# Hybrid decoder step on one core: Pool mixing in three rounded passes, and two token blocks of the second layer fetched and split in the last output tile

## The reference

```python
h = rms_norm(x, g);  z = h @ W_in            # layer 0: 4096 columns, layer 1: 7168
branch = pool_mix(u)            # layer 0: trailing mean over 16, 8, 4 or 2 rows, minus the row,
                                # then per group of 384 channels a 384x384 product, and a scale
branch = stick_breaking(q, k, v)                # layer 1
y = concat(branch * silu(gate), mem_attn(mq) * silu(mgate)) @ W_out;  x = x + y
```

## Time and profile before

| | |
|---|---|
| runs | 2331.37, 2334.32, 2334.16 us; median 2334.16 |
| profiled execution | 2338.4 us, span 2336.7 us |
| mean granted TensorE clock | 0.971 of 2.4 GHz |
| TensorE matmul busy | 2201.2 us (94%) |
| VectorE busy | 1292.6 us (55%) |
| ScalarE busy | 1009.2 us (43%) |
| GpSimd busy | 433.0 us (19%) |

### The profile page before, as it was taken

The page is one execution under the profiler, slowest core; times in us unless marked ns, Lnnn a source line. Parts: engine busy times, 40 slices in busy tenths (PEclk is TensorE's granted clock), DMA queues, the critical chain, the costliest instruction groups (busy, mean ns, idle before and its releaser), DMA issues. The chain is left out here.

```text
span 2336.7 us, 47103 instructions
## 1 busy us (share of the span) xinstructions
PE 2201.2 (94%) x18709; PEld 1834.6 (79%) x18709; DVE 1292.6 (55%) x2040; ACT 1009.2 (43%) x2090; POOL 433.0 (19%) x542
## 2 busy tenths in 40 slices
PE   7799999997999689999999998889999999998999
PEld 6799899886688589999999997766666566654787
DVE  6846666435422374334444443588888888875211
ACT  7533223215311144333333343457777777775100
POOL 0533223202000043222222221321121111100000
PEclk9899999998899889999999999889999999999999
DMA  8222222144635553334433336789999999978331
GB/s 289 86 87 89 79 64 66 66 166 163 210 119 155 146 186 102 109 99 133 153 106 109 96 96 234 253 292 379 396 407 393 406 395 388 375 284 307 123 108 55
DMA packets 283274, 453.98 MB, mean 194 GB/s; under 512 B 30962, under 2 KB 208062, under 8 KB 283038
## 3 DMA queue, kind: packets, MB, share of 16 engines
q1 hardware_dynamic: 274958, 421.83, 51.8%
q0 software_dynamic: 8000, 29.10, 3.3%
q10 hardware_dynamic: 96, 0.02, 0.0%
HBM read 372.43 MB, written 78.43 MB: 193 GB/s over the span
## 5 line engine op out<-in xcount | busy, mean ns | idle before, releaser
L233 DVE TENSOR_TENSOR h_w_lo<-l_w,h_w_hi 128x512 fp32r<-128x512 f32 x264 | 213.7, 811 | 221.2 <-ACT h_w_hi L226 218.7
L226 ACT ACTIVATE h_w_hi<-l_w 128x512 fp32r<-128x512 f32 x264 | 166.7, 633 | 239.9 <-PE i_c L322 81.4
L320 PE MATMUL i_x<-h_t_hi,h_w_hi 128*128 128x264 f32 x560 | 163.3, 292 | 6.8 <-DVE h_t_lo L279 6.8
L2960 PEld LDWEIGHTS b_krow<-ar_arena,b_qd 128*32 128x32 f32 x3072 | 107.2, 111 | 72.6 <-issue 57.0
L192 POOL TENSOR_TENSOR h_w_lo_full<-l_w 128x512 f32<-128x512 f32 x44 | 57.5, 1308 | 560.5 <-DMA l_w<-in_w_in_sb_dram 229.9
L320 PE MATMUL i_y<-h_t_hi,h_w_hi 128*128 128x264 f32 x560 | 161.3, 288 | 0.0
L322 PE MATMUL i_x<-h_t_hi,h_w_lo 128*128 128x264 f32 x560 | 161.0, 287 | 0.0
L321 PE MATMUL i_x<-h_t_lo,h_w_hi 128*128 128x264 f32 x560 | 160.4, 286 | 0.0
L321 PE MATMUL i_y<-h_t_lo,h_w_hi 128*128 128x264 f32 x560 | 159.0, 284 | 0.0
L322 PE MATMUL i_y<-h_t_hi,h_w_lo 128*128 128x264 f32 x560 | 158.9, 284 | 0.0
L2960 PE MATMUL b_krow<-ar_arena,b_qd 128*32 128x128 f32 x3072 | 140.7, 279 | 7.9 <-ACT b_kev L2666 6.9
(11 more groups left out here) (368 smaller groups left out, 6424.9 us busy)
## 6 DMA issues: line engine op xcount, KB each, us to landing
ar_arena<-in_cache_sb_k_dram SPq DMA_DIRECT2D x73, 768.0 KB, 9.7
bf_vpage<-in_cache_sb_v_dram SPq DMA_DIRECT2D x64, 768.0 KB, 8.8
b_vpage<-in_cache_sb_v_dram SPq DMA_DIRECT2D x64, 768.0 KB, 8.5
l_w<-in_w_in_sb_dram SPq DMA_DIRECT2D x56, 512.0 KB, 3.9
l_w<-in_cache_sb_k_dram SPq DMA_DIRECT2D x36, 768.0 KB, 9.4
l_w<-in_w_in_pool_dram SPq DMA_DIRECT2D x32, 512.0 KB, 4.2
bf_kpage<-in_cache_sb_k_dram SPq DMA_DIRECT2D x19, 768.0 KB
ar_arena<-scratch_yT SPq DMA_DIRECT2D x14, 1024.0 KB, 6.6
```

Of the source, the lines that this page charges most:

```text
L226: act.activation(self.w_hi[:, i % RING, :, :], self.source(i), ACT.Copy).then_inc(self.high, 1)
L233: dve.tensor_tensor(self.w_lo[:, i % RING, :, :], self.source(i), self.w_hi[:, i % RING, :, :].bitcast(F32), ALU.subtract).then_inc(self.r ...
L320: pe.matmul(out, w_hi, t_hi, start=kk == 0 and x in ("P1", "P2", "P5"), stop=False, skip_group_check=True)
L2960: ins = pe.matmul(krow[pair * CT:(pair + 1) * CT, 0:P], qd[:, i % 2, at:at + CT], kt[u % 2][:, h, f, :], start=odd == 0 and f == 0, stop=o ...
```

## The change

In layer 0 the ring of split weights has 6 places instead of 8 (5 products ahead instead of 7); the two free places hold the rounded mixing weights and the tail rows. The mixing is done in three rounded passes of 352 columns (81 matmuls a group instead of 27 fp32 ones). ScalarE rounds the mixing weights (`mix_weights`) and the pooled values in three pieces (`mix_high`), VectorE takes the rests (`mix_low`). The evictions go by token third first. `group(n)` moves behind P2 of the next group's first pair. The queries are fetched in two parts, head 0 only when the last mixing matmul is done.

In layer 1 the first pair begins P1, P2, P5. The first weights a(0), in a place of their own, and token blocks 0 and 1 are fetched in the last output tile, split by ScalarE and VectorE ahead of that tile's residual sum, and P1 and P2 run at the end of the output phase, the last tile's transposes between the two halves of P2. `in_phase` begins with P5.

```diff
@@ Quads
+        self.ring = PLACES if i else PLACES - 2
+        self.ahead = self.ring - 1
...
-            self.seq += [(p, "P5")] + [(p - 1, "P4")] * (p > 0) + [(p, x) for x in ("P1", "P2", "P6", "P3", "P7")]
+            begin = [(p, "P5"), (p - 1, "P4"), (p, "P1"), (p, "P2")] if p else [
+                (0, x) for x in (("P1", "P2", "P5") if i else ("P5", "P1", "P2"))]
+            self.seq += begin + [(p, x) for x in ("P6", "P3", "P7")]
@@ pool_phase, SyncE
-                memory.queries(sp)
+                memory.queries(sp, 1, MH)
+                memory.scales(sp)
+                sp.wait_ge(s["mready"], 9 * GROUPS)
+                memory.queries(sp, 0, 1)
                 memory.own_keys(sp)
@@ pool_phase, ScalarE
+                def mix_weights(n):
+                    act.wait_ge(s["wgl"], 16 * (n + 1))
+                    if n:
+                        act.wait_ge(s["mready"], 9 * n)
+                    for kk in range(GB):
+                        act.activation(wg_hi[kk], wg[:, kk, :], ACT.Copy).then_inc(s["wgh"], 1)
+
+                def mix_high(n):
+                    act.wait_ge(s["pooled"], GB * (n + 1))
+                    for u in range(NT):
+                        if u >= 2:
+                            act.wait_ge(s["mready"], 9 * n + 3 * (u - 1))
+                        act.activation(up_hi[u % 2], up[:, :, HIST + u * TT:HIST + (u + 1) * TT], ACT.Copy
+                                       ).then_inc(s["uph"], 1)
...
+                        for n in range(1, GROUPS):
+                            if p + 1 == first(n):
+                                mix_high(n - 1)
                         if p + 1 < q.n:
                             begin(p + 1)
...
+                mix_high(GROUPS - 1)
@@ pool_phase, VectorE
+                def mix_low(n, u):
+                    dve.wait_ge(s["uph"], NT * n + u + 1)
+                    cols = slice(HIST + u * TT, HIST + (u + 1) * TT)
+                    dve.tensor_tensor(up_lo[:, :, cols], up[:, :, cols], up_hi[u % 2].bitcast(F32), ALU.subtract
+                                      ).then_inc(s["upr"], 1)
@@ pool_phase, TensorE
-                                ins = pe.matmul(aux[(at + 1) % 2][:, 0:TT], wg[:, kk, m * P:(m + 1) * P],
-                                                up[:, kk, HIST + u * TT:HIST + (u + 1) * TT], start=kk == 0, stop=kk == GB - 1)
+                                cols, rows = slice(HIST + u * TT, HIST + (u + 1) * TT), slice(m * P, (m + 1) * P)
+                                ins = product3(pe, aux[(at + 1) % 2][:, 0:TT], wg_hi[kk][:, rows], wg_lo[:, kk, rows],
+                                               up_hi[u % 2][:, kk, :], up_lo[:, kk, cols], kk == 0, kk == GB - 1)
...
-                        if n and (p, x) == (first(n), "P1"):
+                        if n and (p, x) == (first(n), "P2"):
                             group(n - 1)
@@ out_phase, SyncE
+                        if t == N - 1:
+                            sp.wait_ge(s["ready"], 2 * (N - 1))
+                            sp.wait_ge(s["dead"], 1)
+                            q.load_a(sp, 0)
+                            for n in range(2):
+                                q.token_fetch(sp, S["tok"], n)
@@ out_phase, ScalarE and VectorE
+                    if norm and t == N - 2:
+                        act.wait_ge(s["dead"], 1)
+                        act.wait_ge(s["ready"], 2 * (N - 1))
+                        act.wait_ge(s["ylo"], N)
+                        for n in range(2):
+                            q.round(act, n)
+                            q.token_high(act, n)
...
+                    if norm and t == N - 2:
+                        for n in range(2):
+                            q.remainder(dve, n)
+                            q.token_rest(dve, n, n + 1)
@@ out_phase, TensorE
                 if norm:
+                    pe.wait_ge(s["added"], 2 * (N - 1))
+                    q.product(pe, 0)
+                    pe.wait_ge(s["sadded"], 1)
+                    q.product(pe, 1, range(1))
                     norm.turn(pe, N - 1)
+                    q.product(pe, 1, range(1, 2))
@@ in_phase
-                q.load_a(sp, 0)
-                for t in (0, 1):
-                    q.token_fetch(sp, S["tok"], t)
                 q.load_b(sp, 1)
...
-                for i, (p, x) in enumerate(q.seq):
+                for i, (p, x) in list(enumerate(q.seq))[2:]:
                     q.product(pe, i)
```

More of the change, by code:

```diff
@@ L217, in round @@
         p, x = self.seq[i]
-        if i >= RING:
-            act.wait_ge(self.done, 2 * (i - RING) + 2)
+        if i >= self.ring:
+            act.wait_ge(self.done, 2 * (i - self.ring) + 2)
         if x in ("P1", "P2"):
@@ L296, in tokens_vector, with product @@
             self.token_rest(dve, t, n)
-    def product(self, pe, i):
+    def product(self, pe, i, halves=range(2)):
         p, x = self.seq[i]
@@ L660, in _ @@
                 act.wait_ge(s["made"], 12)
-                for j in range(3):
+                for j in range(2):
                     q.round(act, j)
@@ L664, in _ @@
                 evacuate(7)
-                q.round(act, 3)
                 act.wait_ge(s["made"], 14)
-                for j in range(4, 6):
+                for j in range(2, 6):
                     q.round(act, j)
@@ L1028, in pool_phase @@
         state = k.sb("state", [NB_S * HIST, GW])
[L1029 removed]
+        tail = spare(q.w_full)[0:KEPT, GW:2 * GW]
         q.allocate_banks(k)
[L1031 to L1032 removed]
+        aux = q.aux
+        names = "gated zeroed keeps stl sturned wgl mready mixed pooled sums tailt tailc stored ystored carried wgh wgr uph upr".split()
         s = {n: k.sem(n) for n in names}
@@ L1070, in _ @@
                 for i, (p, x) in enumerate(q.seq):
-                    q.loads(sp, i + AHEAD - 1)
+                    q.loads(sp, i + q.ahead - 1)
                     if x == "P4" and p < 4:
@@ L1238, in _ @@
                 q.tokens_vector(dve, 0)
-                for j in range(6, AHEAD):
+                for j in range(6, q.ahead):
                     q.remainder(dve, j)
@@ L2105, in _ @@
                     q.token_fetch(sp, S["tok"], t)
-                for j in range(AHEAD - 1):
+                for j in range(q.ahead - 1):
                     q.loads(sp, j)
                 for i, (p, x) in enumerate(q.seq):
-                    q.loads(sp, i + AHEAD - 1)
+                    q.loads(sp, i + q.ahead - 1)
                     kind, h = kinds[p]
@@ L2142, in _ @@
             def _(gp):
-                for j in range(AHEAD + 1):
+                for j in range(q.ahead + 1):
                     q.combine(gp, j)
                 for i, (p, x) in enumerate(q.seq):
-                    q.combine(gp, i + AHEAD + 1)
+                    q.combine(gp, i + q.ahead + 1)
                     if (p, x) in ((0, "P4"), (1, "P4")):
```

226 lines of the change are left out of this document (144 added, 82 removed).

## The result

| | before | after |
|---|---|---|
| median | 2334.24 us (2331.4 to 2342.8) | 2360.28 us (2359.8 to 2361.6) |
| ratio, 95% interval | | 1.0119 [1.0098, 1.0139] |
| profiled execution | 2338.4 us, span 2336.7 | 2360.1 us, span 2358.4 |

What follows compares the result with a forecast made beforehand. TensorE, busy 2201 of 2337 us, was taken to bound the kernel. The terms -1 - 0.6 + 2 + 2.4 + 4.2 + 5 = +12.0 us on 2334.2 gave 2346 us, range 2333 to 2357.

Steps and rivals of the forecast that it cites:

- the join of the layers: Between output phase and second layer: stage starts 13.6 us later, 7.9 comes back; taken as +5 us (-1 to +8).
- what comes back: Second stage of layer 1: P7 27.0 us into the stage instead of 34.9, 7.9 us earlier (6 to 9).
- nothing catches up: Attention start: its own loads are issued behind the Pool stage's barrier, so the +4.2 us delay stays.
- The mixing itself: Pool stage mixing: 81 rounded matmuls at 0.16 us, 12.9 us a group instead of 16, 3.1 saved.
- The gain meets the state load: Pool groups 1 to 3: transposes wait for the state's load, leaving 0.2 us saved each, -0.6 us (-3.6 to +0.6).
- The clock behind the gaps: Behind Pool groups 1 to 3: 5 us gaps bring TensorE's half clock behind all three, +2 us (0 to +4).
- The last group: Last Pool mixing: starts 4.0 us late behind rounding, ends 0.9 late, begins at half clock, +2.4 us (0.5 to 3).
- the join to the attention: Pool stage end: head 0's fetch waits for the last mixing matmul, GpSimd's padding and barrier for it, +4.2 us.
- The Pool start: Start of Pool stage: with six ring places VectorE splits fewer weight blocks between awaited token blocks, -1 us (-2 to +1).
- The early fetches: Rival at the layer join: early fetches land at once and the joins hide, 2329 to 2333 us, chance 0.09.
- The shorter ring: Rival in the Pool stage: six ring places starve TensorE, adding 11 us, 2357 us, chance 0.07.
- The steady clock: Rival in the Pool stage: full clock after 5 us gaps, mixing 11.9 us a group, +2.6, 2337 us, chance 0.14.

Runs made afterwards that it cites:

- Run 2: The changed kernel with the Pool state fetched as soon as its buffer's transposes are done, ahead of the previous group's stores: 2344.6 us.
- run 8: The kernel before with the Pool state fetched ahead of the stores of the group before: 2323.4 us.
- run 3: The changed kernel with all four heads of queries fetched together before the last group: 2361.7 us.
- run 4: The changed kernel with all queries fetched before the last group and the own keys fetched behind that group's stores: 2355.3 us.
- run 6: The changed kernel with the early splits behind tile 7's square, norm and sums, and P1 and P2 at the second stage's start: 2348.2 us.
- run 7: The changed kernel, mended: state and all queries fetched early, own keys behind last stores, splits behind tile 7's chain, P1 and P2 in second stage: 2324.6 us.

## Why the prediction was right in direction and short in size

Set on the profiled executions, the terms are 9.7 us short. By the first table +5.5 lie in the join of the layers, +2.9 in the attention, +2.0 in groups 1 to 3 and +0.4 in the output phase, less 1.2 in the rest. Two steps failed in their mechanism, what comes back at the join of the layers and "nothing catches up" at the attention; in the others a size was off.

**The mixing itself, 12.9 us a group.** 13.65 us, 81 matmuls at 0.161 (forecast 0.16) and what remains until the last is done. The step held, 0.7 us short; against the 16.1 of the fp32 group 2.5 us are saved instead of 3.1.

**The gain meets the state load, -0.6 for three groups.** It held within its bounds (-3.6 to +0.6). From a group's first matmul to the transposes, with the 2.9 us of the product added, it was 22.1, 21.1 and 21.1 us (277.89 less 258.71, and so on), where 20.9 was forecast and 21.2, 21.7 and 21.0 stood before: +0.4. Run 2 shows the load to be the cause. I called the transposes bound by the load without asking why the load goes out so late; run 8 shows that question to be worth 10 us in the kernel before.

**The clock behind the gaps, +2.** The half clock came behind all three. The groups' stretch grew by 3.4 us, 0.4 of it the gap itself, which leaves 3.0 for the clock, inside the bounds of 0 to 4. Of these, 21 more matmuls at the half clock make 2.1; the slower transposes in front of them make up the rest.

**The last group, +2.4, and the join to the attention, +4.2.** Together 6.7 us, forecast 6.6, which is partly luck. The group started 4.1 us later behind the last product (forecast 4.0) and took 15.1 instead of 16.15, so it ended 3.0 late, and the join took 3.7 us more. The second term's reason was half of the truth: head 0's place was free (run 3), and the stores stood in the same queue. The step that failed is "the attention's own loads are issued behind this barrier, so nothing catches up": they are issued behind the landing of the last group's stores as well, and these had moved with the late fetches. Runs 3 and 4 show both halves. Missed: 2.9 us, part of it through the clock behind the longer wait.

**The join of the layers, +5.** It was +10.5, the largest miss. The way to the stage's start was right: 15.2 us later, forecast 13.6. The step that failed is what comes back. "P7 at 27.0, 7.9 us earlier" became 28.6, 6.3 earlier, and then 1.6 went to the wait at the next P5. I took token block 3 to be what P7 waits for and did not follow ScalarE's order through P5's copy, which holds the banks that P3 needs. P3 waited 3.57 us for that copy, P7 then ran right behind P3, and the next P5 waited 2.76 us for an addition of VectorE's. Of the miss of 5.5 us, 1.6 lie in the start, 1.6 in P7, 1.6 in the next P5, and 0.7 in rounding 5.7 down to 5 with "the rate may be a little better".

**The Pool start, -1.** -1.1 by the table, but not shown for its reason: TensorE's wait at the sixth product (P7) fell from 2.1 us to 0.35, and one of 1.8 for an addition of VectorE's came at 116.67, where the stage stood 0.5 us behind. The gain came later, from the clock: the same products took 1.4 us less, at 1.00 after the change and 0.95 before. No trace shows that the change has a part in that, so the agreement is luck. The stretch of before, then that of after:

```profile
164.50:198.00 33.50, 33.50 (x265) 33.50 (x265) 13.63 (x20) 17.65 (x33) 7.26 (x6) 0.95 0.30 95
```

```profile
164.90:197.00 32.10, 32.10 (x266) 32.10 (x266) 10.26 (x20) 17.44 (x32) 7.76 (x6) 1.00 0.35 118
```

**The base.** I subtracted the 4.2 us by which the profile of before lay above its runs. The profile after lies at its own median. The sum, set on the profiled execution, was 2350.4; measured 2360.1. So 9.7 us of the miss of 14 are terms, and 4.3 are this step. In which stages the profile of before lies above its own median is not shown.

**The rivals.** The early fetches did not land at once: weights at 813.4, block 0 at 816.1, 9.7 us behind the issue at 806.4, where 8.7 was forecast. The shorter ring starved nothing that the waits show; the ring was not run by itself. The steady clock did not come with gaps of 5 us.

## What to carry to other kernels

Where a wait is to be priced, ask first why its releaser starts when it does: three waits that I took as given were a fetch standing behind stores in one queue, and moving it alone was worth as much as the whole change, mended. An operation done early costs what stands behind it in every in-order queue that it passes, the stores' landing and the bank copies included; put it behind the chain that ends the phase, even if its data are there. And a stage's start is bound by all engines' last work before the barrier: when one late path is cut, the next can be close behind, half a microsecond in run 3 and 1.1 us in run 6. Last, before a change is credited with a gain, put its best single move into the kernel before (run 8).

## What the runs showed of the hardware

A rounded matmul of 352 columns starts 0.161 us behind the one before. The Trainium skill (TensorE: Matmul & The Clock Gate, "Wait — 56ns, not 53.3ns?") gives columns over 2.4 GHz and 2.5 ns between starts, by which 0.149 us is the estimate. The trace does not agree; the row decides, as it did for 264 columns (0.122 against 0.1125).

TensorE's granted clock stood at 0.50 (1.2 GHz) behind gaps of 4.6 and 5.5 us in the profile after and at 1.00 (2.4 GHz) behind gaps of 0.8 us in runs 2 and 7, at the same three places. Before it was 1.00 behind 2.15 us and 0.50 behind 2.66, but also 0.50 behind 1.92 us at the third group, from the tenth matmul of 264 columns on:

```profile
440.36 0.53 PE L1270 MATMUL p_aux<-c_ident,p_state 120*128 120x120 f32 x3 [1.92 <-DMA p_state<-in_state_pool_dram]
...
441.86:443.36 1.50, 1.50 (x8) 1.50 (x8) 0.00 (x0) 0.39 (x1) 0.00 (x0) 0.50 0.00 0
```

So the length of a gap alone does not order these rows. The fall in the Pool start of before came with no gap in front: from 165.3 to 168.6 the clock stood at 0.50 for 15 matmuls, while TensorE's instructions followed each other without idle time, among them, from 162.4 to 164.3, the one-column matmuls of the queries' squares (L980, L983). After the change the same work kept 1.00.
